# A two-block transformer kernel: the second output projection in PSUM banks that the merge leaves early, and modulation sums spread over other ticks

## The reference

```python
def adaln(cvec, w_mod, b_mod):
    return jnp.split(jax.nn.silu(cvec) @ w_mod + b_mod, 6, axis=-1)

def merge_branches(attn_o, four_o, g_a, g_f, w_pa, w_pf, w_out):
    m = jax.nn.sigmoid(g_a) * (attn_o @ w_pa) + jax.nn.sigmoid(g_f) * (four_o @ w_pf)
    return m @ w_out
...
        sh1, sc1, gt1, sh2, sc2, gt2 = [m[:, None] for m in adaln(c, w_mod[l], b_mod[l])]
        csh1, csc1, cgt1, csh2, csc2, cgt2 = adaln(c_ctx, w_mod[l], b_mod[l])
        h = modulate(rmsnorm(x, g_pre1[l]), sh1, sc1)
        ...
        y = merge_branches(attn, fourier_mix(f), g_a, g_f, w_pa[l], w_pf[l], w_out[l])
        x = x + gt1 * rmsnorm(y, g_post1[l])
        h2 = modulate(rmsnorm(x, g_pre2[l]), sh2, sc2)
```

## Time and profile before

| | |
|---|---|
| median of 3 runs | 1509.76 us (1503.7 to 1515.1) |
| the profiled execution | 1508.69 us, of which 1506.5 us is the span from first to last instruction |
| mean granted TensorE clock | 0.971 of full speed |
| PE busy | 1420.1 us, 94% |
| DVE, ACT, POOL busy | 813.1, 619.8, 57.7 us |
| DMA | 147.68 MB, mean 98 GB/s |

### The profile page before, as it was taken

How to read it: one execution, slowest core, us unless ns; L and a number is a source line. 1 busy time by engine, 2 the same in 40 slices (tenths; PEclk the granted TensorE clock), 3 DMA queues, 4 the chain that set the end, 5 groups by cost and what they waited for, 6 DMA issues and landing times.

```text
span 1506.5 us, 16155 instructions
## 1 busy us (share of the span) xinstructions
PE 1420.1 (94%) x6484; PEld 1106.3 (73%) x6484; DVE 813.1 (54%) x1106; ACT 619.8 (41%) x928; POOL 57.7 (4%) x46
## 2 busy tenths in 40 slices
PE   7989987799999999999989999899889999999995
PEld 5667665575888888888676777687748888888884
DVE  5574666476776667333736655436354443444334
ACT  5345556433545534333523444244343333333332
POOL 3000000002001200000100000000010000000001
PEclk9899999799999999999999999999999999999998
DMA  6422102250322233322033323323312333333221
GB/s 231 168 82 93 57 29 84 99 182 25 116 98 86 97 98 125 127 98 84 28 134 112 102 95 112 99 70 104 134 42 84 98 98 98 98 98 98 98 84 56
DMA packets 41397, 147.68 MB, mean 98 GB/s; under 512 B 4427, under 2 KB 5451, under 8 KB 40940
## 3 DMA queue, kind: packets, MB, share of 16 engines
q1 hardware_dynamic: 41324, 146.66, 28.9%
HBM read 143.23 MB, written 3.41 MB: 97 GB/s over the span
## 4 chain that ended last, share of the span: by engine, by line
PE 83%; DVE 7%; ACT 5%; issue 2%; DMA 2%; SPq 0%; DVEq 0%; ACTq 0%
PE PS L269 25%; PE PS L271 24%; PE PS L270 24%; DVE X L1434 1%; PE PS L877 1%; DVE macc L1434 1%; ACT whi L230 1%; DVE wlo L237 1%; ACT L L1002 1%; PE PS L866 1%; PE PS L438 1%; PE PS L454 1%; PE PS L532 1%; DVE Z L1434 1%; PE PS L561 1%
## 5 line engine op out<-in xcount | busy, mean ns | idle before, releaser
L237 DVE TENSOR_TENSOR wlo<-raw,whi 128x1024 fp32r<-128x1024 f32 x210 | 259.1, 1239 | 434.1 <-ACT whi L230 433.3
L269 PE MATMUL PS<-Hhi,whi 128*128 128x512 f32 x1032 | 414.3, 401 | 17.6 <-DVE wlo L237 6.7
L270 PE MATMUL PS<-Hlo,whi 128*128 128x512 f32 x1032 | 404.3, 392 | 0.0
L271 PE MATMUL PS<-Hhi,wlo 128*128 128x512 f32 x1032 | 404.1, 392 | 0.0
L230 ACT ACTIVATE whi<-raw 128x1024 fp32r<-128x1024 f32 x210 | 220.7, 1055 | 277.9 <-DMA raw<-in_w_up 120.0
L269 PEld LDWEIGHTS PS<-Hhi,whi 128*128 128x128 f32 x1032 | 195.0, 189 | 75.5 <-issue 22.9
L271 PEld LDWEIGHTS PS<-Hhi,wlo 128*128 128x128 f32 x1032 | 194.9, 189 | 41.8
L270 PEld LDWEIGHTS PS<-Hlo,whi 128*128 128x128 f32 x1032 | 195.2, 189 | 39.6 <-issue 1.2
L269 PE MATMUL PS<-Dhi,whi 128*128 128x512 f32 x352 | 136.9, 389 | 0.0
L270 PE MATMUL PS<-Dlo,whi 128*128 128x512 f32 x352 | 136.9, 389 | 0.0
L271 PE MATMUL PS<-Dhi,wlo 128*128 128x512 f32 x352 | 136.9, 389 | 0.0
(11 more groups left out here) (370 smaller groups left out, 1864.5 us busy)
## 6 DMA issues: line engine op xcount, KB each, us to landing
raw<-in_w_up SPq DMA_DIRECT2D x88, 512.0 KB, 3.4
raw<-in_w_down SPq DMA_DIRECT2D x44, 512.0 KB, 3.4
wm<-in_w_mod SPq DMA_DIRECT2D x36, 512.0 KB, 4.1
raw<-in_w_g SPq DMA_DIRECT2D x16, 512.0 KB, 3.4
mw<-in_w_mod SPq DMA_DIRECT2D x3, 2048.0 KB, 8.3
raw<-in_w_o SPq DMA_DIRECT2D x8, 512.0 KB, 3.5
raw<-in_w_out SPq DMA_DIRECT2D x8, 512.0 KB, 3.4
X<-in_x SPq DMA_DIRECT2D x4, 512.0 KB, 8.9
```

Of the source, the lines that this page charges most:

```text
L237: e.tensor_tensor(wlo[i % NS], raw[i % NS], whi[i % NS].bitcast(f32), ALU.subtract).then_inc(q["w_lo"], 1)
L269: e.matmul(o, lhs[0], rhs[0], start=first, stop=False)
L270: e.matmul(o, lhs[0], rhs[1], start=False, stop=False)
L271: return e.matmul(o, lhs[1], rhs[0], start=False, stop=last)
```

## The change

It does these things.

- **OUT_BANK.** The chunks of the second output projection go to banks 6, 7, 4, 5, 0, 1, 2, 3 in place of o mod 5. Chunk 0 no longer waits for the merge's last read (`mg_ab` 16) but for the bias addition of group 8 (`mod`), chunk 1 for the gates' last copy, chunks 2, 4 and 6 for `mg_ab` 12, 14 and 16. The waits for `p_y` go, and one for `p_y` 20 comes before group 11's first part.
- **Splits in the merge.** In o = 7 ACT and DVE no longer split two chunks first; they do it after the merge.
- **mod_sum.** From group 4 on the groups alternate between the two halves of `macc`; a group waits for the columns of the group before the last.
- **A_MOD, A_COLUMNS.** The sums are 2 in each of 17 ticks, then 3 and 3; the columns of groups 4 to 7 come in v = 1, 3, 5, 7. Those of group 8 come before the merge's products, their bias addition and two gains after DVE's first merged tile.
- **W_MOD.** In the first output projection the eight chunks have 4, 4, 5, 5, 5, 5, 4, 0 operations in place of 4 each.
- **SP's order there.** `load_to` runs one chunk less far before each `mod_load`.

```diff
+    def mod_sum(g, v):
+        return (macc2 if g == 3 else macc)[:, v if g < 4 else g % 2, :]
...
-    A_MOD = [3, 3, 2] + [2] * 12 + [4, 4]
-    A_COLUMNS = {0: 4, 2: 5, 4: 6, 6: 7, 7: 8}
+    A_MOD = [2] * 17 + [3, 3]
+    A_COLUMNS = {1: 4, 3: 5, 5: 6, 7: 7}
...
+    W_MOD = [4, 4, 5, 5, 5, 5, 4, 0]
+    OUT_BANK = [6, 7, 4, 5, 0, 1, 2, 3]
...
         for n in range(10, 16):
-            load_to(e, ld, CH["w_o"] + NS + n - 9)
+            load_to(e, ld, CH["w_o"] + NS + n - 10)
             mod_load(e, n)
...
+        e.wait_ge(q["a_olo"], 8)
+        e.wait_ge(q["mod"], MOD_NTH[7])
+        acc_columns(8, 6, 0)
...
         for o in range(8):
             if o == 0:
-                e.wait_ge(q["mg_ab"], 16)
-            if o >= 5:
-                e.wait_ge(q["p_y"], 16 + o - 4)
+                e.wait_ge(q["mod"], MOD_NTH[8])
+            elif o == 1:
+                e.wait_ge(q["g_ev"], 16)
+            elif o % 2 == 0:
+                e.wait_ge(q["mg_ab"], 10 + o)
...
-                last = products(e, PS[:, o % 5, :], wtile(CH["w_out2"] + o, k), (MGhi[:, k, :], MGlo[:, k, :]),
+                last = products(e, PS[:, OUT_BANK[o], :], wtile(CH["w_out2"] + o, k), (MGhi[:, k, :], MGlo[:, k, :]),
...
         e.wait_ge(q["l_mw"], 48)
+        e.wait_ge(q["p_y"], 20)
         mod_group_part(2, range(0, 2), 5)
-        e.wait_ge(q["g_ev"], 16)
         post_stat(2, 7)
...
-            if o % 2:
+            if o % 2 and o < 7:
                 split_to(CH["w_p"] + o + 1 + AHEAD)
...
+        split_to(CH["w_out2"] + AHEAD)
...
-                        e.wait_ge(q["mcol"], MOD_NTH[n // 4 - 1])
+                        e.wait_ge(q["mcol"], MOD_NTH[n // 4 - (2 if n // 4 > 4 else 1)])
...
-            mod_part(4)
+            mod_part(W_MOD[o])
...
-            split_to(CH["w_p"] + (o + AHEAD if o % 2 == 0 else o + 1 + AHEAD))
+            if o < 7:
+                split_to(CH["w_p"] + (o + AHEAD if o % 2 == 0 else o + 1 + AHEAD))
...
+            if o == 0:
+                mod_add(8, 6, 0)
+                tt(P1, MOD[:, 16:24, 0], vc("h_post1", n=8), ALU.mult, "gains")
+                e.wait_ge(q["mod"], MOD_NTH[8])
+                stt(G2, MOD[:, 32:40, 0], 1.0, vc("h_pre2", n=8), ALU.add, ALU.mult, "gains")
```

More of the change, by code:

```diff
@@ L453, in acc_columns @@
                 for v in range(mod_vectors(g)):
-                    last = e.matmul(PS[:, bank, at + 2 * n + v:at + 2 * n + v + 1], (macc2 if g == 3 else macc)[:, v, 128 * n:128 * n + 128],
+                    last = e.matmul(PS[:, bank, at + 2 * n + v:at + 2 * n + v + 1], mod_sum(g, v)[:, 128 * n:128 * n + 128],
                                     ones[:, 0:1], start=True, stop=True)
@@ L956, in tensor_program @@
         e.wait_ge(q["l_mw"], 48)
+        e.wait_ge(q["p_y"], 20)
         mod_group_part(2, range(0, 2), 5)
-        e.wait_ge(q["g_ev"], 16)
         post_stat(2, 7)
         mod_group_part(2, range(2, 8), 5)
-        e.wait_ge(q["a_olo"], 8)
-        e.wait_ge(q["mod"], MOD_NTH[8])
         for c in range(8):
@@ L1383, in scalar_program @@
             split_to(CH["w_out2"] + o + AHEAD)
-            post_chunk(2, o, o % 5, "w_done", CH["w_out2"] + o + 1)
+            post_chunk(2, o, OUT_BANK[o], "w_done", CH["w_out2"] + o + 1)
         ln_exp(e)
@@ L1545, in mod_part @@
                 c, x = csil[:, 2 * k + v:2 * k + v + 1], wm[n % 2][:, j, :]
-                o = (macc2 if n // 4 == 3 else macc)[:, v, :]
+                o = mod_sum(n // 4, v)
                 if i == 0:
@@ L1806, in vector_program @@
                 mod_part(A_MOD[t])
-        e.wait_ge(q["mod"], MOD_NTH[8])
-        tt(P1, MOD[:, 16:24, 0], vc("h_post1", n=8), ALU.mult, "gains")
-        stt(G2, MOD[:, 32:40, 0], 1.0, vc("h_pre2", n=8), ALU.add, ALU.mult, "gains")
         for n in range(16):
```

## The result

| | before | changed |
|---|---|---|
| median, 20 runs each | 1507.64 us (1503.32 to 1515.1) | 1512.46 us (1508.79 to 1518.09) |
| ratio, 95% interval | | 1.0027 (1.0015 to 1.004) |
| span of the profiled execution | 1506.5 us | 1510.2 us |
| mean granted clock | 0.971 | 0.967 |

The change costs 0.27%, 4.1 us by the ratio (2.3 to 6.0): within 1%, on the slower side. Twenty runs of before have a median 2.1 us under that of the three known at the prediction.

The account below looks back on a forecast made before the run. PE, busy 94% of the span, was taken to bound the kernel, so its stops count in full. Terms 13.3 - 4.0 - 7.8 = +1.5 us on the 1509.76 us median gave 1511.3 us, range 1498 to 1519.

Parts of the forecast that it names:

- First output projection: First block's output projection: SP's new order makes piece 15 ready at 349.6, columns of group 3 late: +13.3 us.
- The chain: SP's loads, first output projection: each chunk waits for sums behind the previous chunk's split; six turns of 7.5 us plus sums.
- The landing: Each turn in the first output projection: a 512 KB chunk lands 4.3 us after SP's issue.
- The sums: DVE in the first output projection: sums that free the next pieces, 0.68 us each, 12.2 us together.
- The start: First output projection: the first piece is freed at 292.4, as before.
- Window attention: Window attention stage: removed stops give -10.6 us, late piece 35 costs +6.6; together -4.0 us.
- The gain of the removed stops: Window attention: waits for `macc` in ticks 3 and 17 and three short ones go, -10.6 us.
- The price of piece 35: End of window attention: piece 35 behind `w_pa`'s first chunk delays `ABlo` 5.2 us, slow clock adds 1.4: +6.6.
- Second output projection: Second block's output projection: chunk 0 starts at once, waits before its last k; chunk 1 begins at 1059.1: -7.8 us.
- Rival 1: First output projection: loads are in time and SP's chain does not bind; sum -16 us, 1493.8 us; chance 0.10.
- Rival 2: First output projection: same chain, landings averaging over 4.6 us, 8.3 for the last; sum +9 us, 1518.8; chance 0.12.
- Rival 3: Second output projection: last k starts no earlier because ACT or DVE is late; sum +4.9 us, 1514.7; chance 0.08.

Follow-up runs that it names:

- a_sp9: Changed kernel with SP's old order in the first output projection alone (weight chunks one further before each modulation piece): 1489.15 us, ratio 0.9885 to the kernel before.
- b_sp10: Kernel before with SP's new order in the first output projection alone, four sums per chunk as before: 1532.1 us, ratio 1.0165.
- b_again: Kernel before, unchanged, traced a second time: 1506.55 us in one run, span 1504.4 us.
- a_cap19: Changed kernel with only piece 35 of `w_mod` put before the first chunk of `w_pa` in SP's order: 1508.94 us, ratio 1.0013 to the kernel before.
- b_banks: Kernel before with the second output projection's new banks and waits, the two splits left inside the last merge step: 1504.41 us, ratio 0.9992.
- a_amod: Changed kernel with the old `A_MOD` (sums per tick of the window attention), alternating halves and new `A_COLUMNS` kept: 1505.77 us, ratio 0.9989 to the kernel before.
- best1: Changed kernel with both SP's old order in the first output projection and the old `A_MOD`: 1481.58 us, ratio 0.9835 to the kernel before.
- b_splits: Kernel before with only the two splits moved behind the last merge step, banks as before: 1502.38 us, ratio 0.9971.
- b_out2: Kernel before with the second output projection's part alone (new banks, new waits, two splits moved behind the merge): 1498.79 us, ratio 0.995.

## Why the prediction was right, and where its terms were off

1511.3 us were predicted, 1512.46 measured, inside the range and within 1% of before, as forecast. Part of that closeness is luck. The shift predicted was +1.5 us, the shift measured +4.1, and its interval of 2.3 to 6.0 leaves the +1.5 out; the start, 1509.76, was 2.1 us over the median of twenty runs and made up for it.

**First output projection, +13.3 predicted, +16.4 between the two traces.** The chain is shown: SP's pairs, DVE idle between them, one stop of 10.8 us, and the whole of it gone with one line (a_sp9). The same chain made 24.9 us alone (b_sp10). Three terms were too small. The landing: ACT's six splits in the chain start 4.57, 4.33, 4.50, 4.56, 4.83 and 4.55 us after their chunks' issue, on average 4.56 and not 4.3, which makes 1.6 us over the six turns. The sums: from the first to SP's next issue, or to PE's columns, 12.7 us and not 12.2. The start was 0.1 late. That gives 351.8 for 349.6. The fourth is a step that the prediction left out: behind the longer stop the clock stays low longer, and the part of group 9 takes 6.87 us where it took 5.92, so that the first product is 16.4 us late and the columns 15.5. How much this is worth depends on the trace it is held against: from the start of the columns to the next product are 14.0 us in the changed kernel, 13.0 before and 11.5 in b_again.

The formula of the Trainium skill (DMA: Bandwidth & Descriptors, "Anatomy of one DMA — SWDGE (gpsimd) path") gives an estimate of 4.0 us for such a landing, and it is given there for GpSimd's path. This trace does not agree with it for loads that SP issues in pairs: 4.33 to 4.83 us. The advice of the Trainium skill (the same page, "Rules for kernel authors") to issue a DMA early and wait for it late agrees with a_sp9 and b_sp10: the one line that issues the chunks later is worth 22.8 and 23.9 us of this stage.

Against an execution like b_again the term is 81.5 - 62.9 = 18.6 us: the trace on which the sum was built had 2.2 us of slow clock in this stage that the four other traces with this code lack. This term carries the whole miss in the shift: 3.1 us between the two traces and 2.2 more against b_again, of which the other stages give some back.

**Window attention, -4.0 predicted, -4.6 measured** (-5.4, and +0.8 for group 8's columns behind it). Both parts had the right mechanism. The gain of the removed stops was put at 10.6: the ticks are 12.5 us shorter, 11.7 after group 8's columns, and 1.6 of it comes from the moved sums, which the prediction gave no gain. The price of piece 35 was put at 6.6, as 5.2 of delay and 1.4 of slow clock: the small products take 7.1 us more, 5.4 and 1.7. The stop was 5.41 us, and the clock fell as said, with a mean of 0.57 from 991 to 996; five steps of `ABlo` are the 0.64 us apart that the prediction took. The prediction named the wrong releaser for part of it: it had piece 35 wait for the chunk of `w_pa` alone, and a_cap19 shows that without this chunk 3.16 us of the stop remain, for the sums of piece 33.

**Second output projection, -7.8 predicted, -8.2 measured.** Right in every step: no wait before chunk 0, one of 1.05 us (1.1 predicted) before the last k, full clock. From the first multiplication of the last tile to the end of `MGlo` it took 3.4 us, as before. From the last product of the merge to the first of chunk 1 are 14.8 us before and 7.0 now, -7.8 as predicted. The other 0.4 us was no part of the prediction: before, the merge's products stopped for a split,

```profile
1011.48 0.47 PE L269 MATMUL PS<-FOhi,whi 128*128 128x512 f32 x1 [0.27 <-DVE wlo L237]
```

and in the changed kernel, where the columns of group 8 stand ahead of them, they don't. What the prediction did not see is that the banks alone are worth much less than their share (b_banks).

**Sum.** 16.4 - 4.6 - 8.2 = +3.6 between the traces, 3.7 with the rest. Rival 1 (the chain does not bind, -16 us) is what a_sp9 became: -17.3 by the ratio. Rival 2, longer landings, was to decide over an average of 4.6 us. There was luck in this too. The trace of the changed kernel was at 4.56, but a_amod and a_cap19, whose code there is the same, were at 4.71 and 4.70, over the line: their fifth landing took 5.72 and 5.58 us, and their first projections 82.8 and 82.7 us. It cost 1.3 us only, since the 8.3 us that this rival took for the last landing was in none of them (4.54 to 4.57). Rival 3 fell: the last `MGlo` was earlier.

## What to carry to other kernels

Where one in-order queue alternates loads with different gates, follow back what each load waits for. If that leads over a load further up the same queue, the queue runs at the latency of a whole loop (here 8.8 to 10.5 us a turn against 5.4 us of work), and one place further ahead in the order opens it. A stop behind which the clock falls has a price beyond its length (here 7.1 us for one of 5.4), and a stop that is shortened, but behind which the clock still falls, saves less than it was shortened by; edits that shorten the same stop should be tried together. Where a sum of a few us rests on stages with short stops, take these stages from more than one trace.

## What was not expected of the hardware

The time of the same code behind short stops varies between executions, and stages show it where medians hide it. Seven traces have the old window attention, with stops of 2.5 and 2.9 to 3.8 us in ticks 3 and 17, and took 215.5, 217.8, 217.9, 218.0, 219.0, 221.9 and 223.8 us. The four without these stops agree in pairs: 212.4 and 212.5 (changed, a_sp9), 206.8 and 206.9 (best1, a_amod). The shortest and the longest of the seven differ most behind the stop of tick 17, which is 2.90 us in b_splits and 3.78 in b_out2. The granted clock of the 4 us from about 1 us after it is at the upper level in the first and at the lower in the second (windows of b_splits and b_out2, columns as above); in b_again, with the same 3.78 us, it is 0.57 from 969 to 973 and 1.00 from there on:

```profile
966.00:970.00 4.00, 4.00 (x28) 2.86 (x28) 0.87 (x3) 1.33 (x2) 0.00 (x0) 1.00 0.02 4
```

```profile
973.00:977.00 4.00, 4.00 (x19) 2.09 (x19) 0.00 (x0) 0.11 (x1) 0.00 (x0) 0.50 0.01 4
```

Even behind the stop of 0.64 us in tick 15, which all seven have, the clock differs: 1.00 before (944 to 948) and 0.64 in b_out2 in the same window. Why the clock falls, or stays low longer, in one execution and not in the other behind the same stop is not settled by these runs. It follows that the removed stops are worth more on average than in the first trace: over the seven the old stage averages 219.1 us, so that the changed one is 219.1 - 212.4 - 0.8 = 5.9 us better, not 4.6. Means of all traces with the same code give +19.0 for the first projection (82.3 of three against 63.3 of five), -5.9, and -8.2 for the last stage (88.7 of five against 96.9 of four). The sum is +4.9 us, and the ratio says +4.1 (2.3 to 6.0).

The closed chain also shows landing times that vary: six landings between 4.33 and 4.83 us in the changed kernel's trace, but the fifth of the six took 5.72, 5.58 and 5.44 us in the three others with a closed chain (a_amod, a_cap19, b_sp10). Timelines of SP and ACT in a_amod:

```profile
332.37 0.43 SPq L223 DMA_DIRECT2D raw<-in_w_up  x1
...
338.09 1.06 ACT L230 ACTIVATE whi<-raw 128x1024 fp32r<-128x1024 f32 x1 [8.34 <-DMA raw<-in_w_up]
```

Why it is the fifth stays open.
